# Lower weights of a block in one subtraction, and expert rows fetched at an even pace

## What is computed

```python
def peer(h, w_query, sub_keys, expert_u, expert_v):
    # per token and head (8 heads): the 16 best of 128 x 128 experts by product keys
    ...
    e_idx = take(i1, j // 16) * 128 + take(i2, j % 16)
    gate = softmax(best)
    def chunk(tc, ec, gc):
        a = gelu(einsum('cd,chkd->chk', tc, expert_u[ec]))
        w = gc * a
        return einsum('chk,chkd->cd', w, expert_v[ec])
```

## Time and profile before

| what | value |
|---|---|
| runs shown, median (lowest to highest) | 1956.75 us (1951.56 to 1957.51), 3 runs |
| profiled execution, its own time | 1958.53 us |
| its span, first to last instruction | 1956.5 us |
| granted clock of PE, share of full speed | 1.00 |
| busy share of the span: PE, DVE, ACT, POOL | 99%, 85%, 57%, 34% |
| u stage in the span | about 775 to 1368 us |
| v stage in the span | about 1368 to 1956 us |

### The profile page before, as it was taken

One profiled execution on the slowest core, in us unless ns is written; L12 is line 12 of the kernel. 1 busy time (PEld: TensorE's weight loads), 2 busy tenths in 40 slices (PEclk: granted clock), 3 DMA queues, 4 the chain that ended last, 5 costly groups with the idle time before them and its releaser, 6 DMA issues.

```text
span 1956.5 us, 32644 instructions
## 1 busy us (share of the span) xinstructions
PE 1941.3 (99%) x11722; PEld 1764.6 (90%) x11722; DVE 1664.2 (85%) x2523; ACT 1121.8 (57%) x1588; POOL 659.6 (34%) x409
## 2 busy tenths in 40 slices
PE   9999999999999999999999999999999999999998
PEld 8899989998989888999999999999888888888886
DVE  8777778777888777999999999988888988888887
ACT  7665556555677455666565666645555545554554
POOL 0201110011000001877777777675222221223220
PEclk9999999999999999999999999999999999999999
DMA  6745654566455556999999999999999999999997
GB/s 238 254 162 193 203 193 159 185 204 197 157 177 188 185 184 228 333 338 343 327 345 339 335 339 356 328 364 344 359 379 375 382 378 378 380 375 376 376 380 246
DMA packets 137575, 566.50 MB, mean 290 GB/s; under 512 B 44008, under 2 KB 52080, under 8 KB 88112
## 3 DMA queue, kind: packets, MB, share of 16 engines
q1 hardware_dynamic: 87296, 414.05, 57.9%
q0 software_dynamic: 49936, 149.49, 22.9%
q10 hardware_dynamic: 288, 2.36, 0.3%
HBM read 548.31 MB, written 16.88 MB: 289 GB/s over the span
## 4 chain that ended last, share of the span: by engine, by line
PE 90%; DVE 4%; DMA 3%; ACT 1%; issue 1%; SPq 0%; DVEq 0%; ACTq 0%
PE psum L925 27%; PE psum L617 15%; PE psum L902 15%; PE psum L907 10%; PE psum L621 8%; PE psum L603 3%; PE psum L602 3%; PE psum L607 3%; DMA arena<-u_cols 1%; DMA raw<-v_rows 1%; ACT whi L479 1%; DVE wlo L487 1%; DVE xr L487 1%; DVE arena L1813 1%; PE psum L797 1%
## 5 line engine op out<-in xcount | busy, mean ns | idle before, releaser
L473 DVE TENSOR_TENSOR wlo<-raw,whi 128x1024 fp32r<-128x1024 f32 x242 | 296.2, 1232 | 111.7 <-PE psum L621 74.5
L902 PE MATMUL psum<-xr,whi 128*128 128x384 f32 x2048 | 381.0, 337 | 2.2 <-ACT whi L479 2.2
L925 PE MATMUL psum<-whi,xr 128*128 128x512 f32 x1512 | 363.8, 389 | 1.5 <-DVE psum L1916 0.9
L902 PEld LDWEIGHTS psum<-xr,whi 128*128 128x128 f32 x2048 | 351.1, 188 | 3.0 <-ACT whi L479 2.7
L925 PEld LDWEIGHTS psum<-whi,xr 128*128 128x128 f32 x1512 | 283.4, 188 | 61.7 <-DVE psum L1916 1.3
L479 ACT ACTIVATE whi<-raw 128x2048 fp32r<-128x2048 f32 x168 | 321.0, 1911 | 25.0 <-DMA raw<-v_rows 13.8
L617 PE MATMUL psum<-xr,whi 128*128 128x512 f32 x1296 | 330.2, 397 | 0.4 <-issue 0.4
L466 ACT ACTIVATE whi<-raw 128x1024 fp32r<-128x1024 f32 x244 | 250.4, 1053 | 104.1 <-DMA raw<-stream 47.9
L1364 POOL DMA_INDIRECT arena<-v_rows,small x64 | 143.8, 2247 | 395.4 <-DVE arena L1825 391.9
L617 PEld LDWEIGHTS psum<-xr,whi 128*128 128x128 f32 x1296 | 232.4, 189 | 44.3 <-issue 0.8
L487 DVE TENSOR_TENSOR wlo<-raw,whi 128x1024 fp32r<-128x1024 f32 (+1 forms) x126 | 197.7, 1574 | 26.5 <-issue 21.8
(11 more groups left out here) (282 smaller groups left out, 3228.3 us busy)
## 6 DMA issues: line engine op xcount, KB each, us to landing
raw<-stream SPq DMA_DIRECT2D x244, 512.0 KB, 3.3
raw<-v_rows SPq DMA_DIRECT2D x85, 1024.0 KB
raw<-u_cols SPq DMA_DIRECT2D x84, 1024.0 KB
arena<-v_rows SPq DMA_DIRECT2D x43, 1024.0 KB
arena<-u_cols SPq DMA_DIRECT2D x42, 1024.0 KB
gates<-arena POOLq DMA_DIRECT2D x8, 1536.0 KB, 9.6
small<-gates SPq DMA_DIRECT2D x62, 192.0 KB
arena<-x_t SPq DMA_DIRECT2D x4, 544.0 KB, 6.8
```

The source lines that it names most:

```text
L473: nc.vector.tensor_tensor(wlo[:, k % 2 * HALF:(k % 2 + 1) * HALF], raw[:, s * HALF:(s + 1) * HALF], f(whi[:, s * HALF:(s + 1) * HALF]), AL ...
L902: mm(bank(at, 0, 2 * TD), hi_w[:, c * P:(c + 1) * P], z_all[:, :, c, 0:TD // TS, :], start=c == 0, stop=False)
L925: last = mm(at[:, (b * 4 + j * 2 + n) * 512:(b * 4 + j * 2 + n + 1) * 512], weights, src, start=begin, stop=end, skip_group_check=True)
```

## The change

It does two things. In the planner `row_at`, the two paces of the u stage's row products (every 4.2 half blocks, then every 3) give way to one: the first at half block 9, then every 77/20 = 3.85, the last at 251. With the products, their fetches on POOL are planned by the new pace. In DVE's loop over the blocks of the u stage, the two subtractions of 1024 columns of a block, with a `step` between them, become one subtraction of 2048 columns in the place of the first; it releases both halves at its end, and `step(2n + 1)` follows it.

```diff
         def row_at(n):
-            if n < 48:
-                return 6 + n * 21 // 5
             if n < ROWS:
-                return 207 + (n - 48) * 3
+                return 9 + n * 77 // 20
             return 2 * B_U + 8 + (n - ROWS) * (2 * B_V - 20) // ROWS
...
                 step(2 * n)
                 if n < B_U - 1:
-                    lo_part(dve, n + 1, (0,))
+                    lo_part(dve, n + 1, (0, 1))
                 step(2 * n + 1)
-                if n < B_U - 1:
-                    lo_part(dve, n + 1, (1,))
                 if n == B_U - 2:
                     gate_weights(0)
```

## The result

The changed kernel took 1966.7 us (median of 6 runs, 1964.46 to 1969.1), the kernel before 1953.15 us in the same session. The ratio is **1.0057** (95% interval 1.0038 to 1.0076), slower by 11 us; the two medians lie 13.6 us apart, since the ratios here are not quotients of medians. The forecast was 1952.8 us. Single executions at 2391 to 4951 us, one each in experiments 3 and 7 and in the kernel before beside experiments 5 to 8, stand in no time and no ratio of this text. The profiled execution took 1967.27 us, with a span of 1965.2.

The account below looks back on a forecast made before the run. PE was taken as the bound, busy 1941.3 of 1956.5 us, with DVE and DMA nearly full in the u stage. The sum was 1958.53 - 6.7 + 0.7 + 0.3 = 1952.8 us, range 1950.0 to 1958.6.

Parts of the forecast that it names:

- POOL in part 1: With one 2048-column subtraction, POOL's next gather waits for a product slipping at most 1.14 us, but is planned 18 us ahead.
- Rival B: U stage: DVE starts the subtraction over 2.76 us after the copy, PE waits for all 2048 columns; 1970 or 1961; chance 0.06.
- Rival C: U stage: 339 GB/s is the most DMA gives beside the scatters; 16 us slower, 1968; chance 0.04.
- A: U stage: DMA full enough that late loads reappear spread over the stage, ACT copies over 2.24 us late; 1958.6; chance 0.14.
- The gain on DVE: U stage: one subtraction for two gains DVE 0.08 us a block, 10 us, none of it on PE's path by itself.
- The move: Odd half step goes behind the whole subtraction: PE's four waits for DVE go, next loads asked 2.2 us earlier after products.
- 6.7 us of waits: U stage, 784.90 to 1363.21: 6.7 us lost by PE, carried by ten of 125 blocks, all taken as removed.
- part 2: Rows every 3.85 half blocks: the stage end's overload, 382 GB/s where 365 came through, goes; 5.2 us, near 5.9 found.
- The middle: U stage, 864 to 1240: load rate 348 GB/s fits, new waits 0.7 us (bounds 0 and 6.8), DVE at 97.6%.

Follow-up runs that it names:

- experiment 3: The changed kernel with the subtraction cut into two of 1024 columns in a row, in the same place, even pace: 1953.4 us, ratio 0.9990 to the kernel before.
- experiment 7: The changed kernel with the subtraction cut into four of 512 columns in a row: 1966.9 us, ratio 1.0048 to the kernel before.
- experiment 5: The changed kernel with the u stage subtraction's first input taken from PSUM, result meaningless: 1952.75 us, ratio 0.9993 to the kernel before.
- experiment 6: The kernel before with two small POOL memsets behind each of the 192 scatters: 1966.86 us, ratio 1.0061.
- experiment 8: The kernel before with its old row pace and the two subtractions of 1024 columns in a row ahead of the odd half step: 1950.86 us, ratio 0.9975.
- experiment 4: The changed kernel with 64 of its 192 POOL scatters left out: 1951.9 us, ratio 0.9991 to the kernel before.
- experiment 11: Repeat of experiment 8, old pace with two subtractions of 1024 columns in a row, on the same chip as the even pace: ratio 0.9995 to the kernel before.
- experiment 10: Repeat of experiment 3, even pace with two subtractions of 1024 columns in a row, unchanged: ratio 0.9987 to the kernel before.
- experiment 1: The kernel before with the even pace of the rows alone, its two subtractions and the half step between them kept: 1957.57 us, ratio 1.0012.
- experiment 2: The changed kernel with the old row pace, so one subtraction of 2048 columns alone: 1967.46 us, ratio 1.0065 to the kernel before.

## Why the prediction was wrong, step by step

**The step that failed is POOL in part 1.** I wrote that POOL's next gather waits for a product that slips by at most 1.14 us and is planned 18 us ahead, and so held POOL free. Its durations were taken as fixed, and its list was never added up. The row was there: 283.32 of 376 us in POOL's column, to which the 0.3 us in front of each of its 164 instructions adds 49. That is 332 of 376, 88%, with a reserve of 74 us in the stage (593 less 519). The merged instruction costs it 72 us (591 less 519). None of the rivals B, C or A had POOL in it. Rival B reached the right sign, with PE waiting at the first lower matmul, but its cause (products and route pieces in front) wasn't the one: in experiment 4 the subtraction and DVE's order are B's, and the time is 0.9991. The range, up to 1958.6, missed all of it.

**The gain on DVE was right and didn't matter.** One subtraction of 2.28 us stands for two of 1.22, and its successor starts 2.20 us after it, as the earlier trace rows had it.

**The move was right in kind, too large in size.** With both subtractions ahead of the odd step, all of PE's waits of the earlier trace rows are gone in the profile of experiment 11, where PE is busy for 376.00 and 90.00 us. But the gain in time, with the old pace, was 0.05% to 0.25%, where the sum had 6.7 us of waits to win, 0.34%. The term was read from one execution of 1958.53 us, the slowest of the seven that stand beside the result (1949.62 to 1958.53), and I shifted nothing for that although it already stood above all three that I had. I took it that runs differ in just these waits, and that isn't shown. The kernel of experiment 11, in whose profile PE waits for nothing in the u stage, still ran from 1949.02 to 1958.99 us. And the two slowest profiled executions with two in a row (1964.01 us in experiment 3, 1959.22 in experiment 10) lost 2.8 and 3.3 us in 1400 to 1800, in the v stage (PE 397.22 and 396.75 of 400). What sets the kernel before's typical run stays open; only one of its executions has a profile.

**The cause that part 2 gave for the late waits was wrong.** I had 382 GB/s at the end of the stage as an overload, with 365 coming through. With the pace unchanged and the halves together, the same stretch ran at 376 GB/s, a DMA share of 1.03 and PE without a wait (second line above). So 365 was no ceiling but what a PE with waits asks for. The late waits needed two things together, the dense pace and the product between the halves. Without the product they go (experiment 11), and without the dense pace they go too: in experiment 1 PE is busy for 90.00 of 90 us there. But the loss had moved to the middle (1.9 us there), and the time came out at 1.0012. Once the halves are together, the even pace has nothing left to cure.

**The middle was as forecast.** With the even pace and two subtractions the load rate in 864 to 1240 was 344 to 347 GB/s (forecast 348) and PE lost 0.4 to 2.3 us (I had taken 0.7, bounds 0 to 6.8). DVE's share there was up to 371.4 of 376, 98.8%. With the one long instruction and a POOL that isn't full (experiments 4 and 5) the rate was the forecast's 348, and DVE stood at 366.96 and 367.44 us, 97.6% and 97.7% for a forecast of 97.6%. Rival C and its ceiling of 339 are refuted by the same numbers.

## What to carry to other kernels

Before an instruction of one engine is made longer, add up the list of every engine that shares a port with it, with the issue time in front of each instruction, and take that engine's durations as dependent on the change. A helper that is nearly 90% full and waits for buffers only a few us at a time is close to being the bound, though its waits look like slack. And a loss read from one execution should be set against where that execution stands among the runs before it is promised as a gain.

## What was not expected of the hardware

**A wait between POOL and DVE.** 1.55 us for a scatter alone, and up to 2.06 us more when it begins under a subtraction of 2048 columns with both inputs in SBUF. In the kernel before the mean was 0.24 us more, with two of 1024 columns; in the changed kernel 0.55.

**A long wait of PE can cost more than itself.** PE's timeline of the changed kernel and its windows around it (columns as in the earlier trace rows):

```profile
1293.16 2.98 PE L900 MATMUL psum<-xr,whi 128*128 128x384 f32 x16
1299.90 2.38 PE L905 MATMUL psum<-xr 128*128 128x192 f32 x16 [3.75 <-DVE xr L485]
1302.08 4.24 PE L900 MATMUL psum<-xr,whi 128*128 128x384 f32 x16
1306.15 1.93 PE L905 MATMUL psum<-xr,wlo 128*128 128x192 f32 x16
1307.91 2.97 PE L900 MATMUL psum<-xr,whi 128*128 128x384 f32 x16
```

```profile
1290.00:1299.00 9.00, 6.14 (x42) 5.82 (x40) 3.72 (x3) 3.48 (x4) 7.48 (x6) 1.00 1.05 374
1299.00:1308.00 9.00, 8.10 (x49) 8.10 (x50) 8.01 (x6) 2.13 (x2) 7.48 (x6) 0.81 0.89 312
1308.00:1316.00 8.00, 8.00 (x56) 8.00 (x56) 5.14 (x5) 4.68 (x5) 7.02 (x4) 1.00 1.05 397
```

PE waited 3.75 us, then the granted clock of the next 9 us was 0.81, a mean of stretches at 2.4 and at 1.2 GHz, and one set of sixteen upper matmuls took 4.24 us for 2.97. From 1293.16 to 1307.91 are 14.75 us for three sets, two blocks of 4.573 us: 5.6 us lost for a wait of 3.75. In the kernel before, the longest wait was 1.40 us, and the granted clock of the stretch stayed at 1.00. Other waits of PE for the subtraction bear it out in part: in the 4 to 5 us from about the end of one of 3.15 us in the changed kernel, and of ones of 1.76, 2.46 and 3.45 us in experiment 2, the granted clock was 0.66, 0.67, 0.66 and 0.60, while behind one of 1.38 us there and one of 1.77 us in experiment 6 it stayed at 1.00. So the length of the wait alone doesn't tell it.
